# Moving the last chunk's turns, the RWKV state's turn and the third output projection on TensorE

## What is computed

```python
P = xn @ p['w_in']
# prompt: chunked DeltaNet and RWKV recurrences; sample: one step of each
ga, gb = sigmoid(P[..., O_GATE:O_GATE + D_MODEL]), sigmoid(P[..., O_GATE + D_MODEL:])
m = ga * (o_dn @ p['w_up_dn']) + gb * (o_rw @ p['w_up_rw'])
h = h + m @ p['w_out']
x = rmsnorm(h, p['ln2'])
q = (x @ wq).reshape(..., 8 heads, 2, 128);  s = einsum('thpc,hpnc->thpn', q, keys)
# top 16 of each half, top 16 of their sums -> 16 expert rows per head and token
hid = gelu(einsum('thkd,td->thk', u_tab[eidx], x))
y = rmsnorm(h + einsum('thk,thkd->td', gates * hid, v_tab[eidx]), ln_f)
```

## Time and profile before

| | us |
|---|---|
| median of 3 runs | 1175.23 |
| lowest and highest | 1173.37, 1177.82 |
| span of the profiled execution | 1172.6 |

### The profile page before, as it was taken

The page is one execution under the profiler, slowest core; times in us unless marked ns, Lnnn a source line. Parts: engine busy times, 40 slices in busy tenths (PEclk is TensorE's granted clock), DMA queues, the critical chain, the costliest instruction groups (busy, mean ns, idle before and its releaser), DMA issues.

```text
span 1172.6 us, 11379 instructions
## 1 busy us (share of the span) xinstructions
PE 996.6 (85%) x3771; PEld 567.1 (48%) x3771; DVE 713.3 (61%) x1879; ACT 270.4 (23%) x644; POOL 515.8 (44%) x580
## 2 busy tenths in 40 slices
PE   6999998989999998997897777777777777777787
PEld 5886676879998554763443222222222222222221
DVE  1025772985273616994757766766776776677553
ACT  2146544015233012211112111111122111111111
POOL 2000100000000004667577677777767777777763
PEclk9989899989997998998999999999999999999999
DMA  8342022450244516999999999999999999999996
GB/s 282 108 149 72 1 75 53 128 172 5 72 159 144 182 70 244 405 375 344 409 409 400 409 410 409 409 410 400 409 402 405 410 409 409 399 409 409 405 365 267
DMA packets 119785, 334.27 MB, mean 285 GB/s; under 512 B 19088, under 2 KB 33267, under 8 KB 119463
## 3 DMA queue, kind: packets, MB, share of 16 engines
q0 software_dynamic: 76032, 276.86, 60.1%
q1 hardware_dynamic: 43562, 56.64, 14.9%
q10 hardware_dynamic: 132, 0.04, 0.0%
HBM read 326.99 MB, written 5.74 MB: 284 GB/s over the span
## 4 chain that ended last, share of the span: by engine, by line
PE 39%; DMA 28%; DVE 13%; POOL 12%; issue 5%; ACT 2%; SPq 0%; DVEq 0%; ACTq 0%; POOLq 0%
PE bank L1407 37%; DMA sb_all<-in_peer_u,idx 14%; DMA sb_all<-in_peer_v,idx 13%; POOL sb_all L586 12%; DVE sb_all L1127 2%; ACT sb_all L1805 2%; DVE sb_all L2291 1%; DVE sb_all L2288 1%; DMA sb_all<-in_w_in 1%; DVE sb_all L1105 1%; DVE sb_all L1103 1%; DVE sb_all L1107 1%; PE bank L1629 1%; ACT L1805 0%; DVE key_i L1075 0%
## 5 line engine op out<-in xcount | busy, mean ns | idle before, releaser
L1407 PE MATMUL bank<-sb_all 128*128 128x512 f32 (+15 forms) x3462 | 963.0, 431 | 151.3 <-DMA sb_all<-in_peer_v,idx 134.7
L1407 PEld LDWEIGHTS bank<-sb_all 128*128 128x128 f32 (+7 forms) x3462 | 537.1, 186 | 571.9 <-DMA sb_all<-in_peer_v,idx 317.5
L1127 DVE CUSTOM_DVE_ANT_0 sb_all<-sb_all,bank 128x1024 f32<-128x1024 f32 x264 | 314.5, 1220 | 186.1 <-DMA sb_all<-in_peer_u,idx 185.8
L586 POOL DMA_INDIRECT sb_all<-in_peer_u,idx x264 | 251.2, 952 | 219.9 <-DVE idx L1111 103.3
L586 POOL DMA_INDIRECT sb_all<-in_peer_v,idx x264 | 251.7, 954 | 90.0 <-issue 65.0
L1805 ACT ACTIVATE sb_all<-sb_all 128x128 f32<-128x128 f32 (+11 forms) x368 | 145.4, 421 | 559.7 <-PE bank L1407 367.6
L1805 ACT ACTIVATE sb_all<-bank 128x264 f32<-128x264 f32 (+16 forms) x183 | 82.9, 468 | 326.1 <-PE bank L1407 279.8
L621 POOL IOTA sb_all<- 128x54 f32 x1 | 0.2, 183 | 166.2 <-PE bank L1407 166.2
L1397 POOL MEMSET sb_all<- 128x3456 f32 x1 | 3.0, 2984 | 134.3 <-DVE sb_all L2202 134.3
L2085 DVE SCALAR_TENSOR_TENSOR sb_all<-sb_all 128x288 f32<-128x288 f32 x14 | 6.1, 512 | 64.0 <-ACT sb_all L1805 64.0
L1805 ACT ACT_TABLE_LOAD x22 | 28.2, 1283 | 7.5 <-DVE sb_all L2223 3.9
(11 more groups left out here) (231 smaller groups left out, 412.4 us busy)
## 6 DMA issues: line engine op xcount, KB each, us to landing
sb_all<-in_w_in SPq DMA_DIRECT2D x9, 2048.0 KB, 7.9
sb_all<-in_peer_wq SPq DMA_DIRECT2D x4, 2048.0 KB, 17.6
sb_all<-in_w_in SPq DMA_DIRECT2D x5, 1024.0 KB, 5.2
sb_all<-in_peer_u,idx POOLq DMA_INDIRECT x264, 10.7
sb_all<-in_peer_v,idx POOLq DMA_INDIRECT x264, 11.0
out<-sb_all SPq DMA_DIRECT2D x8, 512.0 KB, 4.6
sb_all<-in_w_out SPq DMA_DIRECT2D x2, 2048.0 KB, 8.3
sb_all<-in_x_prompt SPq DMA_DIRECT2D x4, 512.0 KB, 4.0
```

Of the source, the lines that this page charges most:

```text
L586: pool.indirect_dma_start(ring[at % 8], None, table[0], bass.IndirectOffsetOnAxis(ap=idx[:, c:c + 1], axis=0)).then_inc(landed[at % 8], 16)
L1127: v.tensor_tensor_reduce(uring[i % 8], uring[i % 8], x, 1.0, 0.0, ALU.mult, ALU.add, hdot[:, u % 2, j:j + 1]).then_inc(u_free, 1)
L1407: return nc.tensor.matmul(out, lhsT, rhs, start=start, stop=stop, **kw)
```

## The change

- On TensorE the last chunk's two turns go among the sample's state products: `turn_dn` behind head 0, `turn_rw` behind head 1. A wait for the DeltaNet state of the last chunk goes ahead of the products (bank 3).
- The RWKV state's 8 matmuls become `turn_state`, behind the second output projection.
- `project_out(2)` moves from ahead of the first norm's turn to behind `scores(0, 0)`.
- ScalarE copies the state behind row_root(0). `prwo` lies elsewhere. `place_x(6, ...)`, which writes bank 7, waits for the copy, and `turn_keys` no longer does.
- SP sends the state out behind the load of wq0 instead of ahead of out0.

```diff
--- before.py
+++ after.py
@@ -396,8 +396,8 @@
             exp_ready, gexp_done, tap_kb, silu_done, qk_sq, exp2_ready, tap_va, qk_root, tap_vb, conv_ready, vtok_ready,
             silu_v, dec_exp, tok_ready, prw_ready) = series(sem("act_signals"), 1, 2, 1, 14, 4, 2, 12, 1, 4, 2, 1,
             2, 1, 2, 2, 2, 2, 3, 1, 1, 3, 3, 1, 6, 6, 6)
-        svt_ready, sroot, syt_used, gates_ready, pst_ready, oroot, tokd_ready, keys_ready = series(
-            sem("act_signals2"), 6, 1, 1, 1, 1, 1, 1, 4)
+        svt_ready, sroot, syt_used, gates_ready, oroot, tokd_ready, keys_ready, pst_ready = series(
+            sem("act_signals2"), 6, 1, 1, 1, 1, 1, 4, 1)
         xn2T_ready, score_free, query_used = (Signal(sem(n), 0) for n in ("xn2T_ready", "score_free", "query_used"))
         kq_copied = sem("kq_copied")
         rw_branch = sem("rw_branch")
@@ -408,7 +408,7 @@
         svt = view(E + 1152, RH, 6, RN)
-        prwo = view(T + 3072, 8, 64)
+        prwo = view(I4 + 512, 8, 64)
         strw, prod = view(C, 32, 64), view(C + 2048, 16, 64)
         svp = view(C + 3072, 6, 64)
         vhalf, sa, yv = (view(C + 3456 + 32 * i, 32) for i in range(3))
@@ -517,6 +517,9 @@
             sp.wait_ge(dn_s_done, NCH)
             sp.dma_start(p_dn[0, 0].rearrange("h k v -> k h v"),
                          s_dn_p.rearrange("p (h v) -> p h v", h=4)).then_inc(state_sent, 16)
+
+        def emit_rwkv_state(sp):
+
             sp.wait_ge(pst_ready.sem, pst_ready.at(1))
             sp.dma_start(p_rw[0, 0].rearrange("h v k -> v h k"), prwo[0:64]).then_inc(state_sent, 16)
@@ -667,13 +670,22 @@
             def turn_keys():
                 pe.wait_ge(oroot.sem, oroot.at(1))
-                pe.wait_ge(pst_ready.sem, pst_ready.at(1))
                 pe.wait_ge(tokd_ready.sem, tokd_ready.at(1))
                 pe.wait_ge(keys_in.sem, keys_in.at(16))
                 for n in range(4):
                     for q in range(4):
                         ins = nc.tensor.transpose(psv((6, 7, 4, 5)[n], 128, 128, at=128 * q), keysT[:, 4 * n + q, :], ident)
                     ins.then_inc(keys_t, 1)
+
+            def turn_state():
+
+                pe.wait_ge(rw_s_done, NCH)
+                pe.wait_ge(outer_used, 8)
+                for f in range(4):
+                    for s in range(2):
+                        ins = mm(psv(7, 64, 128, at=128 * f), s_rw_p[:, f, 64 * s:64 * s + 64], ident,
+                                 start=s == 0, stop=s == 1)
+                ins.then_inc(pst_t, 1)
             def outer_product(n):
@@ -765,13 +777,14 @@
             pe.wait_ge(up_used, 16)
             pe.wait_ge(merged, 8)
-            for n in range(3):
+            for n in range(2):
                 project_out(n)
+            turn_state()
             turn(0, 128, 4)
             pe.wait_ge(xn2T_ready.sem, xn2T_ready.at(2))
             queries(0, slice(0, 128), 0, lambda q: psv(4 * (q % 2), 128, 128))
             scores(0, 0)
-            for n in range(3, 6):
+            for n in range(2, 6):
                 project_out(n)
             pe.wait_ge(h_used, 4)
             turn(1, 128, 2)
@@ -814,8 +827,6 @@
             step(fn(view(E + 4096, 2 * NX), view(E + 4096, 2 * NX), ACT.Sigmoid))
             step(fn(gates(14), gates(14), ACT.Sigmoid))
             fn(gates(15), gates(15), ACT.Sigmoid).then_inc(gates_ready.sem, 1)
-            act.wait_ge(pst_t, 1)
-            fn(prwo[0:64].rearrange("p h k -> p (h k)"), psv(7, 64, 512)).then_inc(pst_ready.sem, 1)
             act.wait_ge(osq_sum, 1)
             fn(sdv[:, 6, :], psv(6, 128, 32), ACT.Sqrt, scale=1.0 / DK, bias=eps[:, 0:1]).then_inc(oroot.sem, 1)
@@ -898,12 +909,15 @@
                     fn(psv(b + half, 128, 512), src[:, 512 * half:512 * half + 512]).then_inc(x_ready, 1)
             row_root(0, 128)
+            act.wait_ge(pst_t, 1)
+            fn(prwo[0:64].rearrange("p h k -> p (h k)"), psv(7, 64, 512)).then_inc(pst_ready.sem, 1)
             act.wait_ge(consts, 3)
             act.wait_ge(st_sent, 64)
             fn(sc_all[:, 16, :], zero512[:, 0:256]).then_inc(score_free.sem, 1)
             turned(0, 128, 4)
             act.wait_ge(keys_ready.sem, keys_ready.at(4))
             act.wait_ge(outer_used, 8)
+            act.wait_ge(pst_ready.sem, pst_ready.at(1))
             place_x(6, xn2[:, 0, :])
             queried(0, slice(0, 128), 0, lambda q: psv(4 * (q % 2), 128, 128))
             scored(0, 0)
@@ -1326,6 +1340,8 @@
                 if name == "out1":
                     emit_norm_rows(sp)
                     emit_sample_states(sp)
+                if name == "wq0":
+                    emit_rwkv_state(sp)
             emit_peer_io(sp)
         @block.gpsimd
@@ -1777,11 +1793,6 @@
             turn_dn(NCH - 2, 0)
             pe.wait_ge(rw_yt_used, NCH - 2)
             turn_rw(NCH - 2, 1)
-            pe.wait_ge(rw_s_done, NCH)
-            for f in range(4):
-                for s in range(2):
-                    ins = mm(psv(7, 64, 128, at=128 * f), s_rw_p[:, f, 64 * s:64 * s + 64], ident, start=s == 0, stop=s == 1)
-            ins.then_inc(pst_t, 1)
             pe.wait_ge(syt_ready, 1)
             pe.wait_ge(proj_used, 46)
             for f in range(4):
@@ -1789,12 +1800,15 @@
                                           ident[0:NS, 0:NS])
             ins.then_inc(syt_t, 1)
             pe.wait_ge(st_in, 64)
+            pe.wait_ge(dn_s_done, NCH)
             for h in range(DH):
                 for b in range(NS):
                     ins = mm(psv(3, 128, 2, at=2 * (8 * h + b)), st[:, 8 * h + b, :], sd[:, h:h + 5:4, b])
+                if h == 0:
+                    turn_dn(NCH - 1, 2)
+                if h == 1:
+                    turn_rw(NCH - 1, 4)
             ins.then_inc(sdn_mv, 1)
-            turn_dn(NCH - 1, 2)
-            turn_rw(NCH - 1, 4)
             pe_rest(pe, mm, project)
         @block.scalar
```

## The result

The changed kernel takes 1177.58 us (median of 20 runs, 1174.27 to 1179.64). The kernel before, in 20 runs beside them, takes 1173.09. The profiled execution has a span of 1176.5 us against 1172.6.

A forecast was written before the change was run, and what follows sets the result against it. The expert-table gather stage, DMA-bound, was taken to bound the kernel, its start set by TensorE's last output projection. Terms -4.4 + 3.9 + 2.3 = +1.8 us on the 1175.2 median gave 1177.0 us, range 1171.8 to 1180.8.

The forecast's parts named there:

- What sets the end: Gather stage moves at the expert tables' rate; its start, so the end, shifts with TensorE's last output projection.
- Part 1: Last chunk's turns among the sample's products, state's turn taken away: first up projection starts 4.4 us earlier.
- Part 2: Output projections' order: third projection's 6.8 us go behind scores that come 2.9 earlier, so last projection ends 3.9 later.
- Part 3: New pause at the first norm sends TensorE's clock to 0.50, slowing the work behind it: 2.3 us lost, ends 0 and 5.
- The row that I read as nearest: Earlier trace's later pause before 64 records at 136 columns: 10.64 us against 7.87 scaled from full clock, 2.8 lost.
- my discount for the shorter pause: Low-clock loss at the first norm taken as 2.3 us, not 2.8, the new pause being a bit shorter.
- The sum: Shift of TensorE's last output projection: -4.4 + 3.9 + 2.3 = +1.8 us.
- (1): Rival: TensorE's clock holds through the new pause at the norm; shift -0.5 us, 1174.7; 19%.
- (2): Rival: clock stays low through queries and scores, 10.2 us at half speed; shift +4.6 us, 1179.8; 13%.
- (3): Rival: turns among the products keep the clock at 1.00; shift -7.0 to -4.7 us, 1168.2 to 1170.5; 5%.
- (4): Rival: the up projection does not start sooner; shift +6.2 us, 1181.4; 4%.
- (5): Rival: the shift is swallowed in the gather stage; about 1175.2 us; 6%.

The follow-up runs named there:

- third projection back: Changed kernel with the third output projection ahead of the first norm's turn again, behind the state's turn: ratio 0.9984, 1.9 us faster than before.
- only the projection moved: Kernel before with only the third output projection moved behind the scores: ratio 1.0069, 8.1 us slower than before.
- pause filled: Changed kernel with two unread 512-column matmuls between the state's turn and the norm's turn: ratio 1.0017, 2.0 us slower than before.
- only the turns moved: Kernel before with the last chunk's two turns among the sample's products, the state's turn left ahead of them: ratio 0.9974, 3.1 us faster than before.
- top-k first: Changed kernel with VectorE's first top-k ahead of residual(2): ratio 1.0042, 4.9 us slower than before.
- dense work among the products: Changed kernel with seven unread 512-column matmuls among the sample's 32 products: ratio 1.0116, 13.6 us slower than before.
- the last run: Kernel with only the turns moved, head 3's eight products put behind the second up projection: ratio 0.9954, 5.4 us faster than before.

## Why the prediction was right, and where its sizes were off

Forecast: +1.8 us, 1177.0 in a range of 1171.8 to 1180.8, no change at 0.5%. Measured: +3.6 (2.5 to 4.7) and 1177.58. The direction, the mechanism and the class are right; the shift is twice what I gave. That 1177.0 lies within 0.6 us of the median is luck: I started from 1175.23, three runs, where 20 runs give 1173.09, and this 2.1 too much hid most of what the shift lacked.

- **What sets the end.** Right. In every profile the sixth gather waits for the last projection. Its shift against the anchor and the measured change are: changed kernel +3.6 and +3.6; third projection back -1.1 and -1.9; only the projection moved +6.8 and +8.1; pause filled +0.8 and +2.0; only the turns moved -3.2 and -3.1; top-k first +3.6 and +4.9; dense work among the products +15.1 and +13.6. All these lie within the intervals; what is left, up to 1.5 us, I have not traced. The untypical profile of the last run does not fit as it stands: -3.2 against -5.4 (3.6 to 7.3 faster), or -4.8 without the 1.7 us that its state's turn lost.
- **Part 1, -4.4 us.** Mis-sized: 3.2. The idle time went as forecast. The step that failed is the rate of the products: I kept "0.18 us a record", the mean over the old stretch. That stretch had 27 records at about 0.1 in it: 15 in 1.5 us, and 12 in the 1.3 us behind them:

```profile
348.70:350.00 1.30, 1.30 (x12) 0.87 0.98 372
```

  At the low clock a record takes 0.2 (21 in 4 us, above), and after the change the clock fell within 1 us of the first product. So the products took 13.0 us instead of 11.5 and the up projection began 2.8 us sooner and not 4.4; of the missing 1.6 the up projections gave back 0.4. The only-turns-moved run shows what the state's 1.9 us had paid for: head 0 in 1.95 us.
- **Part 2, +3.9 us.** Right: 6.8 for the projection, less 2.9 for the earlier turn of the norm. VectorE's residual(2) stood where I said, and the run with the earlier top-k showed that this costs nothing by itself. That earlier scores bring nothing was right too; in the changed kernel the low clock kept them from coming earlier at all.
- **Part 3, +2.3 us.** The clock fell, at 0.50 until about 430. Mis-sized: 2.6 in the queries (10.03 against 7.41) and 0.3 in the turn (1.33 against 1.04), so 2.9. The filled pause gave back 2.8. The row that I read as nearest had lost 2.8, and my discount for the shorter pause was without ground. The price is no constant, though: the same pause cost the queries 1.4 us in the run with dense work among the products.
- **The sum.** -3.2 + 3.9 + 2.9 = +3.6. The two mis-sized terms, 1.2 and 0.6, make up the 1.8 that were missing.
- **The rivals.** That the clock holds (1) is ruled out for the profiled executions: the changed kernel, the top-k run and the run with only the third projection moved all show 0.50 there. For the other executions no trace tells. The long slow stretch (2) did not come; it was 7 us. For (3) the clock fell among the products in every profile. (4) and (5) did not happen: the up projection began 2.8 us sooner, and the end moved by as much as the gather.
- **What sent the clock down.** The Trainium skill's two statements (TensorE: Matmul & The Clock Gate) pointed apart. By the one in its section on why this matters the clock would have held through this pause, and here it did not: 1.91 us of idle time, 1.33 of transposes and 0.69 idle, and 0.50. Whether the transposes had a part in it, as its Part 4 suggests, no run shows, since none put other work in their place. I had read the earlier trace rows as speaking for Part 4, and that was wrong. There is no transpose in that stretch; the clock fell there after idle time between plain matmuls, waiting for a gather:

```profile
539.40 2.44 PE L1407 MATMUL bank<-sb_all 128*128 128x512 f32 x4 [2.11 <-DMA sb_all<-in_peer_v,idx]
```

  What is shown is that the pause mattered: with work in it the clock stayed up, in the one execution that was profiled.

## What to carry to other kernels

Before moving a step out of TensorE's way, look at the clock of what stands behind it: 1.9 us of dense work ahead of sparse matmuls cost nothing, since the first of these ran at twice the speed. A step that only waits less is no gain if its consumer is not what the next stage waits for; here the norm's turn came 2.9 us sooner, and the last projection moved back by 6.8. Sparse matmuls behind dense ones that have already brought the clock up are worth a try: one run here points to about 2 us, with intervals that still touch.

## What was not expected of the hardware

- 16 records of products with two moving columns take 1.95 us at a granted clock of 1.00 and 3.3 to 3.5 at 0.50. Small as they are, their time follows the clock.
- Seven matmuls of 512 columns among 32 products (0.85 us each at the full clock, by the 6.77 us of a projection, which has eight) did not bring the clock back; it stayed at 0.50 for some 30 us, from about 345.0 to about 375.7.
- Executions differ in where the clock falls, even over the same work. One profiled execution lost 1.7 us in the state's turn, which took 1.96 us at 1.00 in the others that have it there. Two or three microseconds between two single profiles mean little unless they are measured from a common row.
